# Gather of the expert rows with two float32r parts of x in place of three bf16 parts

## The chip, the core and the metric

The kernel runs on one core of one Trainium2 chip. The core has five engines that matter here: PE (TensorE, matrix products; PEld in the profile is its loading of the stationary operand), DVE (VectorE), ACT (ScalarE), POOL (GpSimd) and SP, whose queue issues the large loads. The metric is the device time of one execution in microseconds (us): 1502.05 us for the kernel before, the median of two runs (1501.78 and 1502.33 us).

## The reference

Two transformer layers are computed for two groups of 128 tokens each (g = 0 and g = 1), 1024 features wide. Each layer has an attention part and a mixture of experts. The change is in the second:

```python
s = jax.nn.sigmoid((t @ w_router).astype(jnp.float32))        # 256 tokens x 64 experts
...                                                           # top 4 groups of 8, then top 8 experts
hid = jax.nn.silu(jnp.einsum('td,edf->tef', t, w_gate)) * jnp.einsum('td,edf->tef', t, w_up)
routed = jnp.einsum('tef,efd->td', hid * gates[:, :, None].astype(hid.dtype), w_down)
shared = (jax.nn.silu(t @ ws_gate) * (t @ ws_up)) @ ws_down
```

There are 64 experts with a hidden width of 256. A token has a gate other than zero for 8 of them, so that the kernel needs to compute an expert for its own tokens only. All of it is float32.

## The kernel before

Each layer runs in stages: products for queries, keys and values; attention; the output product; the normalised row h of each token (`pre_norm`) and its transpose hT; the router; the shared expert; and the loop over the routed experts.

**Router.** PE multiplies hT by the router weights (L738), ACT takes the sigmoid (L998), and DVE chooses the experts in a chain of some 45 small instructions, each of which waits for the one before (L1246 to L1339). PE needs this chain twice: for the ranks (L744 to L748, which wait for the chosen mask, `mask_ready`), and for the list of visits (L753). Between them it works on the shared expert's first product (L758).

**The loop over visits.** Experts are handled in pairs. A visit takes one pair and up to 64 tokens for each expert (64 slots an expert, 128 in all). The profiled execution has 66 visits in the loops of the two layers. In one visit PE does, in this order (`visit`):

- `gate_up` (L814): the gathered rows of this visit by the gate and up weights;
- `gather` for the next visit (L789): the 128 chosen rows of x, transposed. The stationary operand is a 128x128 block of x (tokens by features), the moving one the choice of slots `pick` (tokens by 128 slots, ones and zeros). There are 8 blocks of features and 2 groups of tokens. x is float32, and stands as a sum of three bf16 parts in tile `x_parts` (name x3 in the code), so 8 x 2 x 3 = 48 products;
- two transposes of the hidden rows (L833), and `scatter` for the visit before (L806): 8 products of the float32r matrix `put` by the float32r parts y_hi and y_lo of the result;
- `scatter_prep` (L796, L798): transposes of pick for `put`, and the gates of the slots;
- the down product (L845).

DVE and ACT serve it: the gathered rows and the hidden rows are copied out of PSUM (L1380, L1021, L1377, L1023), `slots_of` makes `put` (L1352, L1355), `choose` builds `pick` for a later visit (L1345, L1347), and L1026 and L1387 split the result into y_hi and y_lo. SP loads 6 MB of weights for each visit, as three transfers of 2 MB, two visits ahead. The order of instructions on each engine is the order in which the code is written; semaphores tie the engines.

Two more gathers, one for each layer, stand ahead of the loops, so `gather` runs 68 times.

**The three parts of x** are made once a layer, between `pre_norm` and the loop: ACT rounds h to the first part (L990), POOL subtracts it from h in place (L483), ACT rounds the rest to the second part (`middle`, L995), POOL subtracts that and writes the third (L487). PE waits for all of it (`x3_ready`) ahead of the first gather.

Of the kernel before, what the change touches and what calls it, by code (L numbers as in the profile page):

```python
# [12 lines left out]
NG = 2  # L13
PAST = 128
P = 128
KT = D // P
# [17 lines left out]
SLOTS = 64  # L34
# [63 lines left out]
def program(nc, io):  # L98
# [6 lines left out]
    cursor = [base]  # L105
# [70 lines left out]
    x3 = sb("x_parts", [P, NG, 3, KT, P], bf16)  # L176
    xgT_at = cursor[0]
    xgT = sb("gathered", [P, 2, KT, P])
    pick = sb("pick", [P, 2, NG, 2 * SLOTS + 8], bf16)
    put = sb("put", [P, 2, NG * T], f32r)  # L180
# [21 lines left out]
    cursor[0] = max(experts_end, shared_region)  # L202
# [4 lines left out]
    cursor[0] = max(cursor[0], phase_end)  # L207
# [12 lines left out]
    cmp1 = sb("cmp1", [P, NG, 8, 8])  # L220

# [4 lines left out]
    with ctx:  # L226
        PS = ctx.enter_context(nc.psum_tensor("PS", [P, 8, HALF], f32))

        def sem(name):
            return ctx.enter_context(nc.semaphore(name))  # L230
# [26 lines left out]
        x_hi, x_rest, x_mid, x3_ready = sem("x_hi"), sem("x_rest"), sem("x_mid"), sem("x3_ready")  # L257
# [140 lines left out]
        def _(pool):  # L398
# [33 lines left out]
            for l in range(DEPTH):  # L432
# [46 lines left out]
                for g in range(NG):  # L479
                    blocks = h[:, g, :].rearrange("t (p j) -> t j p", j=KT)  # L480
                    pool.wait_ge(tr_mm, NG * (3 * l + 2) + g + 1)
                    pool.wait_ge(x_hi, NG * l + g + 1)
                    nc.gpsimd.tensor_tensor(blocks, blocks, x3[:, g, 0, :, :], ALU.subtract).then_inc(x_rest, 1)  # L483
                for g in range(NG):
                    blocks = h[:, g, :].rearrange("t (p j) -> t j p", j=KT)
                    pool.wait_ge(x_mid, NG * l + g + 1)
                    nc.gpsimd.tensor_tensor(x3[:, g, 2, :, :], blocks, x3[:, g, 1, :, :], ALU.subtract).then_inc(x3_ready, 1)  # L487
# [6 lines left out]
        def _(pe):  # L494
# [181 lines left out]
            for l in range(DEPTH):  # L676
# [106 lines left out]
                def gather(u, half):  # L783

                    for j in range(4):
                        jj = 4 * half + j
                        for g in range(NG):
                            for part in range(3):
                                last = mm(PS[:, 5 + half, j * P:(j + 1) * P], x3[:, g, part, jj, :], pick[:, u % 2, g, 0:P],  # L789
                                          start=(g, part) == (0, 0), stop=(g, part) == (1, 2), skip_group_check=True)  # L790
                    last.then_inc(S["ga_mm"], 1)
# [58 lines left out]
                pe.wait_ge(x3_ready, NG * (l + 1))  # L850
# [18 lines left out]
        def _(act):  # L869
# [81 lines left out]
            for l in range(DEPTH):  # L951
# [37 lines left out]
                for g in range(NG):  # L989
                    run(x3[:, g, 0, :, :], h[:, g, :].rearrange("t (p j) -> t j p", j=KT), ACT.Copy).then_inc(x_hi, 1)  # L990

                def middle(g):

                    act.wait_ge(x_rest, NG * l + g + 1)
                    run(x3[:, g, 1, :, :], h[:, g, :].rearrange("t (p j) -> t j p", j=KT), ACT.Copy).then_inc(x_mid, 1)  # L995
# [3 lines left out]
                for g in range(NG):  # L999
                    middle(g)  # L1000
# [31 lines left out]
        def _(dve):  # L1032
# [188 lines left out]
            for l in range(DEPTH):  # L1221
# [19 lines left out]
                rows_out(3 * l + 2)  # L1241

# [98 lines left out]
                def choose(u, visit):  # L1341

                    slots = RK[:, :, bass.ds(visit * 2, 2)].unsqueeze(3).to_broadcast([P, NG, 2, SLOTS])
                    iota = C["slot"].unsqueeze(1).unsqueeze(1).to_broadcast([P, NG, 2, SLOTS])
                    v.tensor_tensor(pick[:, u % 2, :, 0:P].rearrange("p g (e s) -> p g e s", e=2), iota, slots, ALU.is_equal)  # L1345
                    pair = visit & (PAIRS - 1)
                    v.tensor_copy(pick[:, u % 2, :, P:P + 6],  # L1347
                                  G3[:, :, :, :].rearrange("p g e k -> p g (e k)")[:, :, bass.ds(pair * 6, 6)]).then_inc(S["picked"], 1)
# [118 lines left out]
```

## Time and profile before

| | |
|---|---|
| median of two runs | 1502.05 us |
| profiled execution, device time | 1498.62 us |
| its span, first to last instruction | 1496.8 us |
| mean granted TensorE clock | 0.962 |
| loop of layer 0, about | 250 to 750 us of the span |
| loop of layer 1, about | 954 to 1486 us |
| PE busy, all lines | 1386.2 us |
| of it: gate and up (L814) | 464.5 us |
| of it: down (L845) | 241.1 us |
| of it: gather (L789), 3264 products | 194.0 us |

Times in the timeline count from the first instruction. The mean duration of a matmul is longer than the distance between two of them, because they are pipelined: the gather's products have a mean of 219 ns, but 48 of them take 2.85 us from the first start to the last end. Therefore the cost of a group is read from starts in the timeline, not from the mean. Full clock is 1.0 in the column PEclk (2.4 GHz), 0.5 is the lower level (1.2 GHz).

### The profile page before, as it was taken

What the parts mean: (1) busy time and instruction counts of PE and PEld (TensorE: products, weight loads), DVE (VectorE), ACT (ScalarE), POOL (GpSimd) and SP (SyncE); (2) the same over time, 40 slices, a digit from 0 to 9 for tenths busy, and PEclk for the clock granted to TensorE, in tenths of its full rate; (3) what the DMA queues carried; (4) which work ended last, traced back from release to release, by engine and by line L of the source; (5) the groups of instructions that cost most, each with busy time, mean ns of one, the idle gap of its engine ahead of it and who ended that gap; (6) DMA issues with size and microseconds to landing.
All of it is one profiled execution on the core that took longest, in us unless ns stands there. A gap on an engine that the chain in (4) does not pass through costs nothing.

```text
span 1496.8 us, 23839 instructions
## 1 busy us (share of the span) xinstructions
PE 1386.2 (93%) x9650; PEld 783.0 (52%) x9650; DVE 457.0 (31%) x982; ACT 339.5 (23%) x607; POOL 81.6 (5%) x97
## 2 busy tenths in 40 slices
PE   3797888999999999999979696999999999999996
PEld 1575654455454554545458574455454554545443
DVE  1534543222222222222263446322222222222223
ACT  1423451111111111111152354111111111111111
POOL 2011040000000000000020204000000000000000
PEclk7799979999999999999989897999999999999998
DMA  9589845999999999999657534799999999999991
GB/s 358 194 299 403 334 194 201 395 411 407 399 398 410 410 404 410 390 413 406 244 182 279 202 132 169 276 391 412 406 392 417 397 407 412 393 417 394 404 413 46
DMA packets 84831, 509.68 MB, mean 341 GB/s; under 512 B 4736, under 2 KB 4736, under 8 KB 33344
## 3 DMA queue, kind: packets, MB, share of 16 engines
q1 hardware_dynamic: 82960, 503.93, 84.1%
q0 software_dynamic: 1840, 5.31, 1.1%
q8 instruction: 22, 0.36, 0.1%
q14 instruction: 9, 0.07, 0.0%
HBM read 506.60 MB, written 2.62 MB: 340 GB/s over the span
## 4 chain that ended last, share of the span: by engine, by line
PE 86%; DVE 4%; DMA 4%; ACT 3%; issue 1%; POOL 1%; SPq 0%; POOLq 0%; ACTq 0%; DVEq 0%
PE PS L814 30%; PE PS L845 16%; PE PS L789 13%; PE PS L637 10%; PE PS L806 8%; DMA weights<-in_w_ada 2%; DMA weights<-in_w_out 2%; PE PS L833 1%; PE PS L758 1%; PE PS L659 1%; PE PS L778 1%; PE PS L738 1%; ACT weights_split L912 1%; DVE h L1121 1%; PE PS L796 1%
## 5 line engine op out<-in xcount | busy, mean ns | idle before, releaser
L814 PE MATMUL PS<-weights,gathered 128*64 128x512 f32 x2112 | 464.5, 592 | 0.0
L814 PEld LDWEIGHTS PS<-weights,gathered 128*64 128x64 f32 x2112 | 151.5, 137 | 301.9 <-issue 301.9
L845 PE MATMUL PS<-weights,hiddenT 128*64 128x512 f32 x1056 | 241.1, 598 | 0.0
L789 PEld LDWEIGHTS PS<-pick,x_parts 128*128 128x128 bf16 x3264 | 182.6, 98 | 54.7 <-issue 54.7
L789 PE MATMUL PS<-pick,x_parts 128*128 128x128 bf16 x3264 | 194.0, 219 | 0.0
L1377 DVE SCALAR_TENSOR_TENSOR hidden<-PS,slot_gate,silu 128x256 f32<-128x256 f32 x66 | 32.0, 485 | 410.5 <-ACT silu L1019 410.5
L1026 ACT ACTIVATE y_hi<-PS 128x512 fp32r<-128x512 f32 x132 | 78.9, 597 | 304.7 <-PE PS L845 304.7
L1387 DVE TENSOR_TENSOR y_lo<-PS,y_hi 128x512 fp32r<-128x512 f32 x132 | 91.3, 692 | 154.1 <-ACT y_hi L1026 154.1
L845 PEld LDWEIGHTS PS<-weights,hiddenT 128*64 128x64 f32 x1056 | 69.9, 136 | 114.5 <-issue 113.1
L637 PE MATMUL PS<-weights_split,hT_high 128*128 128x512 f32 x448 | 110.0, 401 | 14.7 <-ACT weights_split L912 8.9
L1019 ACT ACTIVATE silu<-PS 128x256 f32<-128x256 f32 x66 | 25.4, 384 | 429.7 <-PE PS L814 429.7
L637 PEld LDWEIGHTS PS<-weights_split,hT_high 128*128 128x128 f32 x448 | 85.7, 194 | 36.3 <-issue 9.3
L806 PE MATMUL PS<-y_hi,put 128*128 128x512 f32 x272 | 90.4, 413 | 2.8 <-DVE y_lo L1387 2.8
L806 PE MATMUL PS<-y_lo,put 128*128 128x512 f32 x272 | 84.8, 393 | 0.0
L1380 DVE COPY gathered<-PS 128x512 f32<-128x512 f32 x66 | 45.7, 692 | 123.7 <-PE PS L789 123.7
L415 POOL TENSOR_SCALAR rstd<-sum_squares 128x1 f32<-128x1 f32 x16 | 8.5, 529 | 1169.2 <-ACT h L919 1161.2
L659 PE MATMUL PS<-weights,c_columns 128*32 128x256 f32 x768 | 50.4, 418 | 16.1 <-DMA weights<-in_w_ada 16.1
L1062 DVE TENSOR_TENSOR weights_split<-weights,weights_split 128x4096 fp32r<-128x4096 f32 x14 | 61.6, 4420 | 12.1 <-ACT weights_split L912 12.1
L1352 DVE CAST put<-PS 128x256 fp32r<-128x256 bf16 x68 | 28.9, 425 | 107.1 <-PE PS L798 107.1
L806 PEld LDWEIGHTS PS<-y_lo,put 128*128 128x128 f32 x272 | 51.1, 188 | 11.5
L1021 ACT ACTIVATE gathered<-PS 128x512 f32<-128x512 f32 x66 | 39.4, 597 | 69.5 <-PE PS L789 69.5
L637 PE MATMUL PS<-weights_split,hT_low 128*128 128x512 f32 x224 | 53.1, 389 | 0.0
(227 smaller groups left out, 982.1 us busy)
## 6 DMA issues: line engine op xcount, KB each, us to landing
weights<-in_w_gate SPq DMA_DIRECT2D x66, 2048.0 KB, 9.8
weights<-in_w_up SPq DMA_DIRECT2D x66, 2048.0 KB, 14.2
weights<-in_w_down SPq DMA_DIRECT2D x66, 2048.0 KB, 11.1
weights<-in_w_ada SPq DMA_DIRECT2D x24, 2048.0 KB, 13.9
weights<-in_w_in SPq DMA_DIRECT2D x10, 2048.0 KB, 9.6
weights<-in_w_out SPq DMA_DIRECT2D x4, 2048.0 KB, 16.9
weights<-in_ws_gate SPq DMA_DIRECT2D x2, 1024.0 KB, 4.8
weights<-in_ws_up SPq DMA_DIRECT2D x2, 1024.0 KB, 6.9
```

Source lines behind the costliest of these rows:

```text
L637: last = mm(PS[:, banks[g], :], rows_[:, j, g, :], w[:, j * HALF:(j + 1) * HALF], start=start and j == 0, stop=w is lo and j == KT - 1, sk ...
L659: last = mm(PS[32 * q:32 * q + 32, bank, 0:QUARTER], cb[:, jj, :, :].rearrange("p g c -> p (g c)"), w[:, j, q * QUARTER:(q + 1) * QUARTER] ...
L789: last = mm(PS[:, 5 + half, j * P:(j + 1) * P], x3[:, g, part, jj, :], pick[:, u % 2, g, 0:P], start=(g, part) == (0, 0), stop=(g, part) = ...
L806: last = mm(PS[:, 2 * g + n, :], put[:, u % 2, g * T:(g + 1) * T], y[:, n * HALF:(n + 1) * HALF], start=False, stop=False, skip_group_chec ...
L814: last = mm(PS[64 * e:64 * e + 64, 4, :].rearrange("p (a n) -> p a n", a=2), xgT[:, b, j, 64 * e:64 * e + 64], w[:, e, :, j, :], start=j = ...
L845: last = mm(PS[64 * e:64 * e + 64, bank, :], hidT[:, j, 64 * e:64 * e + 64], w[:, e, j, n * HALF:(n + 1) * HALF], start=j == 0, stop=j == ...
L1021: run(*gathered(1 - b, 0), ACT.Copy).then_inc(S["xg_a"], 1)
L1026: run(yhi[:, n * HALF:(n + 1) * HALF], PS[:, bank, :], ACT.Copy).then_inc(S["yhi_done"], 1)
L1062: v.tensor_tensor(lo, w, hi.bitcast(f32), ALU.subtract).then_inc(w_low, 1)
L1377: v.scalar_tensor_tensor(hid[:, :], PS[:, 4, F:2 * F], slot_gate[:, b:b + 1], silu[:, :], ALU.mult, ALU.mult)\
L1380: v.tensor_copy(xgT[:, 1 - b, 4:8, :], PS[:, 6, :].rearrange("p (j s) -> p j s", j=4)).then_inc(S["xg_d"], 1)
L1387: v.tensor_tensor(ylo[:, cols], PS[:, bank, :], yhi[:, cols].bitcast(f32), ALU.subtract).then_inc(S["ylo_done"], 1)
```

## The change

x now stands as two float32r parts: ACT writes the first (the same place, L990 before), and DVE subtracts it from h and writes the second, right behind `rows_out` and ahead of the router's chain. POOL's four subtractions a layer and ACT's two `middle` roundings are gone. The gather takes both parts, so 8 x 2 x 2 = 32 products, and its moving operand is a new float32r tile `pick_rows`, built by DVE with one more instruction in `choose`. The bf16 `pick` stays for `scatter_prep`. A region of scratch for the router's tiles moves to an unused part of another tile; no wait goes with that.

```diff
--- before.py
+++ after.py
@@ -173,10 +173,11 @@
 
     phase_end = cursor[0]
     cursor[0] = shared_region
-    x3 = sb("x_parts", [P, NG, 3, KT, P], bf16)
+    x2 = sb("x_parts", [P, NG, 2, KT, P], f32r)
     xgT_at = cursor[0]
     xgT = sb("gathered", [P, 2, KT, P])
     pick = sb("pick", [P, 2, NG, 2 * SLOTS + 8], bf16)
+    pickr = sb("pick_rows", [P, 2, NG, 2 * SLOTS], f32r)
     put = sb("put", [P, 2, NG * T], f32r)
     y_at = cursor[0]
     yhi = sb("y_hi", [P, D], f32r)
@@ -199,12 +200,11 @@
     nmx = sb("pair_count", [P, PAIRS])
     act_ = sb("active", [P, VISITS])
     assert cursor[0] <= xgT_at + 8192
-    cursor[0] = max(experts_end, shared_region)
+    cursor[0] = mb_at + 4096
     incl = sb("active_sum", [P, VISITS])
     pos = sb("position", [P, VISITS])
     item = sb("item", [P, 4])
     wsum = sb("gate_sum", [P, 4])
-    cursor[0] = max(cursor[0], phase_end)
     s_ = sb("scores", [P, NG, N_EXP])
     sel = sb("sel", [P, NG, N_EXP])
     selm = sb("sel_masked", [P, NG, N_EXP])
@@ -218,6 +218,7 @@
     gm = sb("group_mask", [P, NG * N_EXP_GROUPS])
     top8 = sb("top8", [P, NG, 8])
     cmp1 = sb("cmp1", [P, NG, 8, 8])
+    assert cursor[0] <= mb_at + 16384
 
     C = {k: const[:, a:a + n] for k, (a, n) in where.items()}
     ident = C["ident"]
@@ -254,7 +255,7 @@
         nwt_mm, nwt_a, nwt_d, npv_mm, cat_done = sem("nwt_mm"), sem("nwt_a"), sem("nwt_d"), sem("npv_mm"), sem("cat_done")
         wo_mm, resid = sem("wo_mm"), sem("resid")
         w_high, w_low = sem("w_high"), sem("w_low")
-        x_hi, x_rest, x_mid, x3_ready = sem("x_hi"), sem("x_rest"), sem("x_mid"), sem("x3_ready")
+        x_hi, x_low = sem("x_hi"), sem("x_low")
         rlog_mm, s_ready, mask_ready, rank_mm = sem("rlog_mm"), sem("s_ready"), sem("mask_ready"), sem("rank_mm")
         item_ready, item_mm, table_ready = sem("item_ready"), sem("item_mm"), sem("table_ready")
         sh_mm, sh_silu, sh_hid, sht_mm, shT_ready = sem("sh_mm"), sem("sh_silu"), sem("sh_hid"), sem("sht_mm"), sem("shT_ready")
@@ -476,15 +477,6 @@
                 nc.gpsimd.memset(ylo[:, :].bitcast(f32), 0.0)
                 nc.gpsimd.memset(put[:, 1, :].bitcast(f32), 0.0)
                 nc.gpsimd.memset(slot_gate[:, :], 0.0).then_inc(cleared, 1)
-                for g in range(NG):
-                    blocks = h[:, g, :].rearrange("t (p j) -> t j p", j=KT)
-                    pool.wait_ge(tr_mm, NG * (3 * l + 2) + g + 1)
-                    pool.wait_ge(x_hi, NG * l + g + 1)
-                    nc.gpsimd.tensor_tensor(blocks, blocks, x3[:, g, 0, :, :], ALU.subtract).then_inc(x_rest, 1)
-                for g in range(NG):
-                    blocks = h[:, g, :].rearrange("t (p j) -> t j p", j=KT)
-                    pool.wait_ge(x_mid, NG * l + g + 1)
-                    nc.gpsimd.tensor_tensor(x3[:, g, 2, :, :], blocks, x3[:, g, 1, :, :], ALU.subtract).then_inc(x3_ready, 1)
                 root(4 * l + 3)
                 if l + 1 < DEPTH:
                     root(4 * l + 4)
@@ -785,9 +777,9 @@
                     for j in range(4):
                         jj = 4 * half + j
                         for g in range(NG):
-                            for part in range(3):
-                                last = mm(PS[:, 5 + half, j * P:(j + 1) * P], x3[:, g, part, jj, :], pick[:, u % 2, g, 0:P],
-                                          start=(g, part) == (0, 0), stop=(g, part) == (1, 2), skip_group_check=True)
+                            for part in range(2):
+                                last = mm(PS[:, 5 + half, j * P:(j + 1) * P], x2[:, g, part, jj, :], pickr[:, u % 2, g, :],
+                                          start=(g, part) == (0, 0), stop=(g, part) == (1, 1), skip_group_check=True)
                     last.then_inc(S["ga_mm"], 1)
 
                 def scatter_prep(u):
@@ -847,7 +839,7 @@
                                           skip_group_check=True)
                         last.then_inc(S["down_mm"], 1)
 
-                pe.wait_ge(x3_ready, NG * (l + 1))
+                pe.wait_ge(x_low, NG * (l + 1))
                 pe.wait_ge(S["picked"], 1)
                 for half in range(2):
                     gather(0, half)
@@ -987,17 +979,10 @@
                 rows_out(3 * l + 2)
                 act.wait_ge(kv_out, 64 * (l + 1))
                 for g in range(NG):
-                    run(x3[:, g, 0, :, :], h[:, g, :].rearrange("t (p j) -> t j p", j=KT), ACT.Copy).then_inc(x_hi, 1)
-
-                def middle(g):
-
-                    act.wait_ge(x_rest, NG * l + g + 1)
-                    run(x3[:, g, 1, :, :], h[:, g, :].rearrange("t (p j) -> t j p", j=KT), ACT.Copy).then_inc(x_mid, 1)
+                    run(x2[:, g, 0, :, :], h[:, g, :].rearrange("t (p j) -> t j p", j=KT), ACT.Copy).then_inc(x_hi, 1)
 
                 act.wait_ge(rlog_mm, l + 1)
                 run(s_[:, :, :], PS[:, 7, 0:NG * N_EXP].rearrange("p (g e) -> p g e", g=NG), ACT.Sigmoid).then_inc(s_ready, 1)
-                for g in range(NG):
-                    middle(g)
                 for g in range(NG):
                     act.wait_ge(sh_mm, NG * l + g + 1)
                     run(ssilu[:, g, :], PS[:, 2 + g, 0:F], ACT.Sigmoid).then_inc(sh_silu, 1)
@@ -1239,6 +1224,10 @@
                     finish_vector(7)
                 pre_norm(4 * l + 2, BCAST * (4 * l + 3))
                 rows_out(3 * l + 2)
+                for g in range(NG):
+                    blocks = h[:, g, :].rearrange("t (p j) -> t j p", j=KT)
+                    dve.wait_ge(x_hi, NG * l + g + 1)
+                    v.tensor_tensor(x2[:, g, 1, :, :], blocks, x2[:, g, 0, :, :].bitcast(f32), ALU.subtract).then_inc(x_low, 1)
 
                 dve.wait_ge(kv_out, 64 * (l + 1))
                 dve.wait_ge(router_in, 32 * (l + 1))
@@ -1342,6 +1331,7 @@
 
                     slots = RK[:, :, bass.ds(visit * 2, 2)].unsqueeze(3).to_broadcast([P, NG, 2, SLOTS])
                     iota = C["slot"].unsqueeze(1).unsqueeze(1).to_broadcast([P, NG, 2, SLOTS])
+                    v.tensor_tensor(pickr[:, u % 2, :, :].rearrange("p g (e s) -> p g e s", e=2), iota, slots, ALU.is_equal)
                     v.tensor_tensor(pick[:, u % 2, :, 0:P].rearrange("p g (e s) -> p g e s", e=2), iota, slots, ALU.is_equal)
                     pair = visit & (PAIRS - 1)
                     v.tensor_copy(pick[:, u % 2, :, P:P + 6],
```

**PE, one visit of the loop**, from `gate_up` to the down product (x_parts is x, pick or pick_rows the choice of slots, put the scatter matrix). Before:

```order
L814 MATMUL PS<-weights,gathered 64x512 x16
L826 REGISTER_ALU
L827 REGISTER_ALU
L789 MATMUL PS<-pick,x_parts 128x128 x48
L833 MATMUL PS<-const,hidden 128x128 x2
L806 MATMUL PS<-y_hi,put 128x512 x2
```

and with the change:

```order
L806 MATMUL PS<-weights,gathered 64x512 x16
L818 REGISTER_ALU
L819 REGISTER_ALU
L781 MATMUL PS<-pick_rows,x_parts 128x128 x32
L825 MATMUL PS<-const,hidden 128x128 x2
L798 MATMUL PS<-y_hi,put 128x512 x2
```

The gather stays in its place and has 32 products for 48; everything else on PE is as it was (line numbers are 8 to 10 lower).

**DVE, the last part of a visit.** Before:

```order
L1380 COPY gathered<-PS 128x512
L1352 CAST put<-PS 128x256
L1355 TENSOR_REDUCE slot_gate<-PS 64x1 x2
L1345 ISA
L1345 TENSOR_TENSOR pick<-const,slot_of 128x2x128
```

and with the change:

```order
L1370 COPY gathered<-PS 128x512
L1342 CAST put<-PS 128x256
L1345 TENSOR_REDUCE slot_gate<-PS 64x1 x2
L1334 ISA
L1334 TENSOR_TENSOR pick_rows<-const,slot_of 128x256
L1335 TENSOR_TENSOR pick<-const,slot_of 128x2x128
```

One instruction is added, ahead of `pick` and of the two y_lo subtractions that follow in both.

**POOL, behind the roots of the norm** (tiles cleared for the loop, then the parts of x, then the next root). Before:

```order
L477 MEMSET put 128x256
L478 MEMSET slot_gate 128x2
L483 TENSOR_TENSOR h<-h,x_parts 128x8x128 x2
L487 TENSOR_TENSOR x_parts<-h,x_parts 128x1024 x2
L415 TENSOR_SCALAR rstd<-sum_squares 128x1
```

and with the change:

```order
L478 MEMSET put 128x256
L479 MEMSET slot_gate 128x2
L416 TENSOR_SCALAR rstd<-sum_squares 128x1
```

POOL has no elementwise work left between the clearing and the next root.

## Rows read from the trace of the kernel before

**Rows 1.** The page: the chain that ended last, by engine and line.

```profile
PE 86%; DVE 4%; DMA 4%; ACT 3%; issue 1%; POOL 1%; SPq 0%; POOLq 0%; ACTq 0%; DVEq 0%
```

**Rows 2.** The timeline of PE, one visit (start us, us, what).

```profile
700.39 7.04 PE L814 MATMUL PS<-weights,gathered 128*64 128x512 f32 x32
707.36 2.85 PE L789 MATMUL PS<-pick,x_parts 128*128 128x128 bf16 x48
710.05 0.46 PE L833 MATMUL PS<-const,hidden 128*128 128x128 f32 x2
...
715.92 7.04 PE L814 MATMUL PS<-weights,gathered 128*64 128x512 f32 x32
```

**Rows 3.** Windows in the loop: PE, PEld, DVE, ACT, POOL busy us, PEclk, DMA share, GB/s.

```profile
490.00:505.50 15.50, 15.50 (x112) 7.86 (x111) 3.71 (x9) 2.56 (x5) 0.00 (x0) 1.00 1.00 415
...
567.50:583.00 15.50, 15.50 (x112) 7.89 (x110) 3.71 (x9) 2.56 (x5) 0.00 (x0) 1.00 0.98 397
```

**Rows 4.** Waits of SP's queue: total us, times, longest.

```profile
SPq L388 <- PE PS L845: 460.1, 62, 7.5
```

**Rows 5.** Groups by form on PEld: xcount | busy us, mean ns | idle.

```profile
L789 PEld LDWEIGHTS PS<-pick,x_parts 128*128 128x128 bf16 x3264 | 182.6, 98 | 54.7 <-issue 54.7
...
L806 PEld LDWEIGHTS PS<-y_lo,put 128*128 128x128 f32 x272 | 51.1, 188 | 11.5
```

**Rows 6.** Line L596, weight loads: duration ns min/median/max.

```profile
L596 PEld LDWEIGHTS PS<-U,probs x32: 186/192/333, 130.5 to 870.4; 128*128 128x128 f32 x32
```

**Rows 7.** The timeline of PE in attention.

```profile
161.97 0.39 PE L596 MATMUL PS<-cache_nv,probs 128*128 128x64 f32 x2
...
163.54 1.92 PE L501 MATMUL PS<-const,h 128*128 128x128 f32 x16
```

**Rows 8.** The timeline of PEld at the scatter.

```profile
710.22 0.32 PEld L806 LDWEIGHTS PS<-y_hi,put 128*128 128x128 f32 x2
```

**Rows 9.** The timeline at the router of layer 0.

```profile
209.89 4.07 ACT L990 ACTIVATE x_parts<-h 128x1024 bf16<-128x1024 f32 x2
...
217.96 0.29 DVE L1246 TENSOR_TENSOR sel<-scores,b_router 128x128 f32<-128x128 f32 x1 [7.87 <-ACT scores L998]
...
219.73 0.29 DVE L1259 TENSOR_TENSOR cmp<-group_score 128x128 f32<-128x128 f32 x1
219.86 5.30 POOL L487 TENSOR_TENSOR x_parts<-h,x_parts 128x1024 bf16<-128x1024 f32 x2 [2.38 <-ACT x_parts L995]
219.94 2.75 DVE L1260 TENSOR_TENSOR cmp<-group_score 128x128 f32<-128x128 f32 x1
222.72 2.59 DVE L1262 TENSOR_TENSOR cmp<-cmp,const 128x128 f32<-128x128 f32 x1
...
228.38 0.20 PE L744 MATMUL PS<-chosen,earlier 128*128 128x64 bf16 x1 [3.89 <-DVE chosen L1285]
...
228.54 7.95 PE L758 MATMUL PS<-weights,hT 128*128 128x512 f32 x14
```

**Rows 10.** Windows behind the chosen mask, layer 0 and layer 1; columns as above.

```profile
230.00:236.40 6.40, 6.40 (x12) 2.33 (x10) 5.07 (x25) 0.10 (x1) 0.00 (x0) 0.77 0.00 0
...
934.70:940.90 6.20, 6.20 (x19) 2.57 (x17) 5.70 (x31) 0.38 (x1) 0.00 (x0) 1.00 0.01 1
```

**Rows 11.** The timeline of layer 0, up to the first gather.

```profile
236.42 0.38 PE L753 MATMUL PS<-const,item 128*1 128x128 f32 x2
...
237.44 0.15 DVE L1347 COPY pick<-gate_parts 128x12 bf16<-128x12 bf16 x1
238.55 2.84 PE L789 MATMUL PS<-pick,x_parts 128*128 128x128 bf16 x48
```

**Rows 12.** The timeline at the router of layer 1.

```profile
934.56 0.20 PE L744 MATMUL PS<-chosen,earlier 128*128 128x64 bf16 x1 [3.70 <-DVE chosen L1285]
...
934.72 6.25 PE L758 MATMUL PS<-weights,hT 128*128 128x512 f32 x14
```

**Rows 13.** The timeline of DVE at the end of a visit.

```profile
713.24 0.42 DVE L1345 TENSOR_TENSOR pick<-const,slot_of 128x256 bf16<-128x256 f32 x1
...
715.05 0.69 DVE L1387 TENSOR_TENSOR y_lo<-PS,y_hi 128x512 fp32r<-128x512 f32 x1 [1.31 <-ACT y_hi L1026]
```

## Prediction

> **What bounds the kernel now.** I read the chain of waits first: 86% of the span ends on PE [rows 1]. The timeline of one visit shows the same: PE goes from `gate_up` to `gate_up` in 715.92 - 700.39 = 15.53 us without an idle time [rows 2], and in windows of the loop it is busy for 15.50 of 15.50 us at full clock [rows 3]. The same windows show a second resource that is almost full: the DMA engines are busy for 98 to 100% and move 397 to 415 GB/s. Which of the two is ahead is read from SP's queue: it waits for the down product 62 times, 460.1 us in all, up to 7.5 us at a time [rows 4], so transfers are asked for when PE lets go of a buffer, and PE does not wait for them. PE is the bound, with the transfers right behind it. A longer gather is therefore paid in full; a shorter one soon meets the transfers. Last I read the stretch around the router, where PE does wait: 3.89 us for the chosen mask in layer 0 [rows 9] and 3.70 us in layer 1 [rows 12].
>
> **The gather, 68 times.** Now it takes PE from 707.36 to 710.05, the start of the next product: 2.69 us for 48 products, 0.056 us each [rows 2]. At that pace 128 columns pass in 0.053 us at 2.4 GHz, so in bf16 the moving columns set the pace, and the weight loads are hidden: their mean is 98 ns, and they overlap [rows 5].
>
> The 32 new products have the same shape, but both operands are float32r, 4 bytes each. The trace has no float32r product with 128 moving columns; those of the scatter have 512. What it has is the weight load: in float32r with 128 columns one takes 188 ns against 98 for bf16 [rows 5]. With 512 moving columns there is room for that. The same load occurs with fewer columns in attention, on plain float32: 186 to 192 ns [rows 6], in front of 64 moving columns. There 14 products lie between 161.97 and 163.54 [rows 7]: 1.57 / 14 = 0.112 us each. In plain float32 a product is recorded as two instructions, and by the other rows such an instruction streams its columns twice (L814 below); 2 x 64 columns at 2.4 GHz are 0.053 us, half of what is seen. So there the pace is set by the loads, at 0.112 us. This is my price for a float32r product with 128 columns: its load is of the same size and length (188 and 192 ns), and its own stream of 0.053 us is hidden behind it.
>
> The bounds: from below 0.056 us, if the loads can be hidden as in bf16; from above 0.13 us, the distance of two float32r loads at the scatter (two of them in 0.32 us, the last 0.19 long [rows 8]), as far as the loads alone set it. A higher price needs another mechanism (rival C). I take 0.112, since the load's duration fits that row within 4 ns.
>
> So a gather takes 32 x 0.112 = 3.58 us, 0.89 more than 2.69. With 68 gathers (66 visits and one ahead of each loop) that is **+60.5 us**. At 0.13 it is 4.16, +100 us. Nothing hides it, since PE has no idle time in the visit [rows 2, 3]. The number of products in the other groups stays the same. L814 also gives the two-pass figure: 32 recorded instructions of 512 columns, two at a time on halves of the array, in 7.0 us, 0.44 us a pair [rows 2].
>
> The Trainium skill, TensorE: Matmul & The Clock Gate, section "Back-to-back issue gap", puts the distance of isolated matmuls at the moving columns over the clock plus some 2.5 ns, 56 ns for 128 columns, and names no type. The bf16 gather agrees with it (56 ns), the float32 rows do not (112 ns). By that rule 32 products would be 1.79 us and the change a gain; that is rival A. The same page, "Weight-path perf modes", says that the fast weight load is not used for FP32 inputs, and "LDWEIGHTS" gives columns / 1.2, 107 ns for 128 columns; by it the sum would be +50 us.
>
> **`choose` on DVE.** One more instruction with 256 elements, like `pick` at 0.42 us [rows 13]. In a visit it pushes the end of pick's group, and behind it the first y_lo subtraction, which today waits for 1.31 us on ACT's y_hi [rows 13]. 0.42 fits; 0. If ACT were earlier by an unexpected 0.9 us, DVE would be late by what is missing, under 0.4 us. The next `gate_up` and gather need `slot_gate` and the pick much later. Ahead of the loop, the first gather needs the pick: between 237.59 (end of the copy, 237.44 + 0.15) and 238.55 there is 0.96 us [rows 11]; 0.42 fits.
>
> **The parts of x, twice.** ACT's first rounding stays (209.89 to 213.96). DVE gets two subtractions of 1024 elements in the time when it waits for 7.87 us, until 217.96 [rows 9]. They have no row on DVE. Behind the rounding of the second group (213.96) there are 4.0 us for the last of them; POOL needs 5.30 / 2 = 2.65 us for such a one [rows 9], and DVE can be expected to need no more: 0. If it took twice that, 1.3 us a layer.
>
> POOL's subtractions go, and this is worth more than their own time. DVE's comparison L1259 takes 0.29 us, while the next two of the same shape take 2.75 and 2.59 us and end as POOL's two subtractions (219.86 to 225.16) end [rows 9]. Without POOL's work I price both at 0.29: the mask is 4.76 us earlier. PE waits for it for 3.89 and 3.70 us [rows 9, 12], so both waits go, and what is late next is PE's own work: **-7.6 us**. In layer 0 the 14 products behind the mask take 7.95 us, in layer 1 6.25 [rows 9, 12], at a granted clock of 0.77 and 1.00 [rows 10]. The drop came after the pause; with none I expect full clock: **-1.7 us**. The bounds are 0 and -9.5 us (twice 4.76). The list of visits (L753) comes after 14 products of PE in which DVE's chain has time.
>
> The Trainium skill, GPSIMD Engine Reference, section "Specifications", says that POOL shares its SBUF interfaces with VectorE and contends with DVE instructions that have two SBUF inputs. L1260 and L1262 agree; the tenfold price is only in the trace.
>
> ACT's two `middle` roundings lie behind the sigmoid, off PE's chain: 0.
>
> **The sum.** 1498.6 + 60.5 - 7.6 - 1.7 = 1549.8 us against the profiled execution. The median of the runs is 3.4 us above that execution (1502.05), so I expect **1553 us**, 3.4% more. A measurement here tells about 2% from no change, 30 us: the lines are 1472 and 1532.
>
> **Rivals.**
>
> A, faster than before: the float32r loads are hidden, a product costs its stream of 0.056 us, and a gather 1.79 us. PE's visit falls to 14.6 us. Then the transfers take over: at the best window's 415 GB/s the 6 MB (6.29 million bytes) need 15.2 us a visit, 0.37 less than now, 66 x 0.37 = 24 us. It gives 1502 - 9 - 24 = 1469 at best, 1484 if the present 15.4 (share 0.99) is the floor. For it: bf16 loads overlap. Against: float32 loads do not overlap so at 64 columns. The change is a gain below 2.69 / 32 = 0.084 us a product, before the router's gain. 0.10.
>
> B, in between: the load is partly hidden, 0.085 to 0.105 us, and the time is 1495 to 1538. No row is of that kind. 0.07.
>
> C, a short float32r stream is handled as plain float32, as two instructions' worth: L753 has 128 moving columns and a single weight column, two instructions in 0.38 us, of which the last is some 0.27 (0.108 a piece, 0.22 a product) [rows 11]. 32 x 0.22 = 7.0 us, +4.3 x 68 = +295, 1788 us. For it: nothing but the missing row at 128 columns. 0.07.
>
> D, the forecast, but POOL is not what held DVE (the two comparisons are slow in themselves): 9 us more, 1562; it is inside the forecast's range. That the change does not do what it says is excluded by the order: 32 products stand there, and the scatter's float32r products are recorded once each (8 a visit).
>
> **Chances and range.** The forecast (0.109 to 0.13 us, with or without the router's gain) has 0.74 and spans 1547 to 1602 us; something else that makes it slower has 0.02. To hold 8 in 10 I take 1512 to 1595: the forecast but its outer end, and the greater part of B. Faster by over 2%: 0.03 (A's best end). Within 2%: A's rest and most of B, 0.13. Slower: 0.84.
>
> **What the profile after should show.** The gather's 32 products in 3.5 to 4.2 us, and weight loads near 188 ns; a visit of 16.4 us with PE busy throughout; the DMA share in the loop near 0.94; L1260 and L1262 (ten lines earlier) at 0.29 us, and PE without a wait ahead of the ranks; y_lo still waiting for ACT, some 0.9 us. A gather near 1.8 us with PE waiting for weights would be A, one of 7 us C. If PE waits inside the visit for `picked` or for DVE, my zero for `choose` is wrong.

## The result

The changed kernel takes 1554.2 us (median of two runs, 1553.72 and 1554.67) against 1502.05 us: 3.5% slower, ratio 1.035 with a 95% interval from 1.032 to 1.038. The forecast was 1553 us. Measured again beside the experiments, the ratio was 1.039 (1.036 to 1.043).

The timeline of PE in the profile after shows one visit (start us, us, what); it answers to [rows 2]:

```profile
714.00 3.79 PE L781 MATMUL PS<-pick_rows,x_parts 128*128 128x128 f32 x32
717.62 0.47 PE L825 MATMUL PS<-const,hidden 128*128 128x128 f32 x2
...
730.48 3.79 PE L781 MATMUL PS<-pick_rows,x_parts 128*128 128x128 f32 x32
```

The gather takes 717.62 - 714.00 = 3.62 us for 32 products, 0.113 us each, where 48 products took 2.69. The visit is 730.48 - 714.00 = 16.48 us for 15.53, with no idle time between.

The group of the gather's loads on PEld (xcount | busy us, mean ns of one | idle), against [rows 5]:

```profile
L781 PEld LDWEIGHTS PS<-pick_rows,x_parts 128*128 128x128 f32 x2176 | 248.2, 192 | 54.5 <-issue 54.5
```

A load for the gather has gone from 98 to 192 ns, the length of the float32 loads of [rows 6].

The timeline at the router of layer 0, against [rows 9, 11] (L730 is the router's product, L750 the shared expert's, L736 the first of the ranks):

```profile
209.48 7.06 PE L730 MATMUL PS<-w_router,hT 128*128 128x64 f32 x32 [1.09 <-DVE hT L1032]
211.05 4.09 DVE L1230 TENSOR_TENSOR x_parts<-h,x_parts 128x1024 fp32r<-128x1024 f32 x2 [1.94 <-ACT x_parts L982]
...
216.33 8.55 PE L750 MATMUL PS<-weights,hT 128*128 128x512 f32 x14
...
216.99 0.29 DVE L1235 TENSOR_TENSOR sel<-scores,b_router 128x128 f32<-128x128 f32 x1 [1.84 <-ACT scores L985]
...
218.96 0.28 DVE L1249 TENSOR_TENSOR cmp<-group_score 128x128 f32<-128x128 f32 x1
219.28 0.29 DVE L1251 TENSOR_TENSOR cmp<-cmp,const 128x128 f32<-128x128 f32 x1
...
224.72 0.19 PE L736 MATMUL PS<-chosen,earlier 128*128 128x64 bf16 x1
...
224.87 6.25 PE L750 MATMUL PS<-weights,hT 128*128 128x512 f32 x14
...
232.78 4.08 PE L781 MATMUL PS<-pick_rows,x_parts 128*128 128x128 f32 x32
```

The two comparisons that took 2.75 and 2.59 us take 0.28 and 0.29. PE has no wait ahead of the ranks (L736), and the 14 products behind them take 6.25 us for 7.95. From the router's first product to the first gather PE now needs 232.78 - 209.48 = 23.30 us; before it was 238.55 - 210.45 = 28.10. In the kernel before, the router's first product in layer 0, and the same and the first gather in layer 1, are

```profile
210.45 7.06 PE L738 MATMUL PS<-w_router,hT 128*128 128x64 f32 x32 [1.09 <-DVE hT L1047]
...
916.63 7.06 PE L738 MATMUL PS<-w_router,hT 128*128 128x64 f32 x32 [1.09 <-DVE hT L1047]
...
943.03 2.84 PE L789 MATMUL PS<-pick,x_parts 128*128 128x128 bf16 x48
```

and in layer 1 after:

```profile
942.41 7.06 PE L730 MATMUL PS<-w_router,hT 128*128 128x64 f32 x32 [1.09 <-DVE hT L1032]
...
964.48 4.08 PE L781 MATMUL PS<-pick_rows,x_parts 128*128 128x128 f32 x32
```

So layer 1 needs 22.07 us for 26.40. Against that, in layer 0 the 14 products ahead of the ranks take 8.55 us for 7.18. Windows of the profile after (PE, PEld, DVE, ACT, POOL busy us, PEclk, DMA share, GB/s) show the clock there:

```profile
216.30:224.70 8.40, 8.40 (x16) 3.59 (x16) 6.23 (x40) 0.28 (x1) 0.00 (x0) 0.72 0.00 1
224.80:231.00 6.20, 6.20 (x20) 2.62 (x18) 5.47 (x28) 0.39 (x1) 0.00 (x0) 1.00 0.00 0
```

The granted clock in this stretch was 0.87 before and is 0.72 now. It is at its lower level through the whole of the router's products in both, and comes back between 219 and 220 us before, at 221 us after.

### The profile page after: what moved, and what is told of

Its sections match the earlier page's. It is cut to its first block, busy times and chain, and to the rows that moved or that the text cites. A ratio compares the mean times of both kernels' runs of the same rounds, so it can differ in the third digit from the quotient of the medians.

```text
span 1551.9 us, 21721 instructions
## 1 busy us (share of the span) xinstructions
PE 1450.3 (93%) x8562; PEld 847.3 (55%) x8562; DVE 479.3 (31%) x1056; ACT 331.8 (21%) x603; POOL 60.3 (4%) x89
## 4 chain that ended last, share of the span: by engine, by line
PE 88%; DMA 3%; ACT 3%; DVE 3%; issue 2%; POOL 1%; SPq 0%; POOLq 0%; ACTq 0%; DVEq 0%
PE PS L806 29%; PE PS L781 16%; PE PS L837 15%; PE PS L629 9%; PE PS L798 8%; PE PS L750 2%; DMA weights<-in_w_ada 2%; DMA weights<-in_w_out 1%; PE PS L825 1%; PE PS L651 1%; PE PS L770 1%; PE PS L730 1%; ACT weights_split L904 1%; DVE h L1106 1%; PE PS L788 1%
## 5 line engine op out<-in xcount | busy, mean ns | idle before, releaser
L781 PEld LDWEIGHTS PS<-pick_rows,x_parts 128*128 128x128 f32 x2176 | 248.2, 192 | 54.5 <-issue 54.5
L781 PE MATMUL PS<-pick_rows,x_parts 128*128 128x128 f32 x2176 | 258.3, 277 | 0.0
## 6 DMA issues: line engine op xcount, KB each, us to landing
weights<-in_w_up SPq DMA_DIRECT2D x66, 2048.0 KB, 14.1
weights<-in_w_ada SPq DMA_DIRECT2D x24, 2048.0 KB, 14.1
```

What stands on the lines that cost most here:

```text
L781: last = mm(PS[:, 5 + half, j * P:(j + 1) * P], x2[:, g, part, jj, :], pickr[:, u % 2, g, :], start=(g, part) == (0, 0), stop=(g, part) == ...
```

## The experiments

Twelve runs were made: ten further kernels, the kernel after once more (after_again) and one of the ten a second time. Several of them leave out a part of the gather, so that only their times are of use. "L" is the theory of the prediction: the load of the stationary operand sets the distance of the gather's products.

### What sets the price of a product

**Half of the moving columns** (moving_64), the kernel after with

```diff
-last = mm(PS[:, 5 + half, j * P:(j + 1) * P], x2[:, g, part, jj, :], pickr[:, u % 2, g, :],
+last = mm(PS[:, 5 + half, j * P:j * P + SLOTS], x2[:, g, part, jj, :], pickr[:, u % 2, g, 0:SLOTS],
```

> The kernel after, with only the first 64 of the 128 slot columns as moving operand of the gather (the other slots are not gathered, so half of the gathered rows are stale). Theory L, the load of 128 columns of 4-byte weights sets the distance: 32 products still take 3.6 us (0.113 each), the visit stays at 16.5 us and the time near 1554 us. Rival S, the float32r stream is slow by itself and costs in proportion to its columns: 0.056 us each, 1.8 us for 32, the visit falls to 14.7 us or to what the transfers allow (15.2 to 15.4), about 1475 to 1485 us.

It took 1687.85 us (one run). The timeline of PE:

```profile
694.43 3.76 PE L781 MATMUL PS<-pick_rows,x_parts 128*128 128x64 f32 x32
698.03 0.60 PE L825 MATMUL PS<-const,hidden 128*128 128x128 f32 x2
698.28 1.20 PE L798 MATMUL PS<-y_hi,put 128*128 128x512 f32 x2
...
712.48 4.46 PE L781 MATMUL PS<-pick_rows,x_parts 128*128 128x64 f32 x32
716.75 0.70 PE L825 MATMUL PS<-const,hidden 128*128 128x128 f32 x2
```

At full clock 32 products lie between 694.43 and 698.03, 0.1125 us each, though each streams half of what it did. This is what L says; the rival S, in which the price goes with the columns, has 1.8 us for the 32. But the total agrees with neither: the gather at 712.48 needs 4.27 us, and the scatter behind the first one has its first two products in 1.20 us for 0.70. Windows of the same run (columns as above) show the clock:

```profile
710.00:715.00 5.00, 5.00 (x35) 3.10 (x31) 0.48 (x1) 0.90 (x2) 0.00 (x0) 1.00 0.81 269
715.00:720.00 5.00, 5.00 (x21) 4.41 (x21) 0.69 (x1) 0.47 (x2) 0.00 (x0) 0.53 0.96 397
720.00:725.00 5.00, 5.00 (x23) 1.90 (x23) 2.18 (x7) 0.60 (x1) 0.00 (x0) 0.78 0.95 401
```

PE is never idle, and yet the granted clock falls from 1.00 to its lower level toward the end of the gather, and comes back in the down product.

The same kernel **once more** (moving_64_again) and one with 96 columns (**moving_96**, `pickr[:, u % 2, g, 0:96]` and 96 output columns) asked whether that was a disturbance:

> The kernel of moving_64 once more (the first 64 of the 128 slot columns alone, half of the gathered rows stale). There the distance of the products at full clock was 0.112 us as in the kernel after, but the granted clock fell in the gather and the time was 1688 us. Theory H, the clock answers to how little the array streams while it waits for loads: again a mean clock near 0.88 and 1650 to 1700 us. Rival N, it was a disturbed run: mean clock 0.966 and 1554 us.

> The kernel after with the first 96 of the 128 slot columns as moving operand of the gather (a quarter of the gathered rows stale). Theory L (loads set the distance): 0.112 us and 3.6 us for 32 where the clock is full. Theory H (the clock falls with little streaming): if it goes with the streamed share, 96 columns lie between 128 (mean clock 0.966, 1554 us) and 64 (0.876, 1688 us), 1554 to 1640 us. Rival N: 0.966 and 1554 us.

The first gave 1684.58 us, ratio 1.122 (1.117 to 1.128), mean clock 0.880. The second gave 1598.9 us (one run), mean clock 0.930 over the run, and 0.113 us a product where the clock is full:

```profile
661.74 3.78 PE L781 MATMUL PS<-pick_rows,x_parts 128*128 128x96 f32 x32
665.35 0.49 PE L825 MATMUL PS<-const,hidden 128*128 128x128 f32 x2
```

So it was no disturbance (N falls), and H, the theory that the clock answers to the products, has its forecasts met: with 128, 96 and 64 columns at the same distance of products, the mean clock is 0.966, 0.930 and 0.88, and the time 1554, 1599 and 1685 to 1688 us. A smaller product made the kernel slower by 130 us. The number of visits is 66 in all of them (2112 records of the gate and up products); what changes is their length. From start to start of `gate_up` a visit takes 16.48 or 18.0 us with 96 columns, and 16.49, 18.0 or 19.57 us with 64, where it is 16.48 or 16.49 us with 128. Stale or wrong values among the gathered rows do not by themselves lower the clock: moving_256 and weights_64 below have them as well, and the mean clock there is 0.970 and 0.963.

**Twice the moving columns** (moving_256), both token groups' slots side by side, into 256 output columns:

```diff
+last = mm(PS[:, 5 + half, (j % 2) * 2 * P:(j % 2 + 1) * 2 * P], x2[:, g, part, jj, :], pickr[:, u % 2, :, :].rearrange("p g s -> p (g s)"),
```

> The kernel after, with 256 moving columns in each product of the gather (the slot columns of both token groups side by side), the same number of products and the same weights; what is gathered is then wrong. Theory L: a stream of 256 columns is 0.107 us at full clock, still just under the load, so the distance rises only a little, to 0.113 to 0.122 us (float32r with 512 columns shows 13 ns above its stream): 3.6 to 3.9 us for 32, time 1554 to 1573 us. Rival S: twice the columns, 0.226 us, 7.2 us for 32, the visit 20.1 us, about 1798 us.

```profile
708.66 7.04 PE L806 MATMUL PS<-weights,gathered 128*64 128x512 f32 x32
715.63 4.04 PE L781 MATMUL PS<-pick_rows,x_parts 128*128 128x256 f32 x32
719.50 0.41 PE L825 MATMUL PS<-const,hidden 128*128 128x128 f32 x2
725.33 7.04 PE L806 MATMUL PS<-weights,gathered 128*64 128x512 f32 x32
```

Twice the work in 3.87 us for 3.62: 0.121 us a product (0.117 to 0.118 between two starts). L holds. The visit grew by 0.19 us to 16.67. The total, 1597.24 us, is above what was expected for another reason: the gather's records number 2240 for 2176, which is two visits more, 33 us. Both are in layer 1 (36 visits for 34; layer 0 has 32 in both), where the router works on the wrong results of layer 0.

**Half of the stationary columns** (weights_64):

```diff
-last = mm(PS[:, 5 + half, j * P:(j + 1) * P], x2[:, g, part, jj, :], pickr[:, u % 2, g, :],
+last = mm(PS[0:64, 5 + half, j * P:(j + 1) * P], x2[:, g, part, jj, 0:64], pickr[:, u % 2, g, :],
```

> The kernel after, with only 64 of the 128 columns of each stationary block of x in the gather (the other 64 rows of each block stay stale). Theory L: the load halves, to about 137 ns in its record as in the expert products with 64 columns, and the distance falls to 0.056 to 0.07 us, 1.8 to 2.2 us for 32. PE's visit would be 14.7 to 15.0 us, and then the transfers set it: 15.2 to 15.4 us a visit, about 1470 to 1485 us. Rival S and any fixed price of a float32r product: the distance stays 0.113 us and the time 1554 us.

```profile
652.07 2.14 PE L781 MATMUL PS<-pick_rows,x_parts 128*64 128x128 f32 x32
...
666.89 2.14 PE L781 MATMUL PS<-pick_rows,x_parts 128*64 128x128 f32 x32
```

With the same 128 moving columns and half of the load, 32 products need (2.14 - 0.22) / 31 = 0.062 us each, about half of 0.113; the 0.22 us is the mean of one product. Together with the runs before, this shows L: with 128 stationary columns the price follows the load and not the stream. The time was 1442.24 us, less than the 1470 expected at the lowest: the floor that I had put on the transfers is not there. The visit is 666.89 - 652.07 = 14.82 us.

**Fewer columns in bf16** (bf16_96): the kernel before with `x3[:, g, part, jj, 0:96]` and 96 output partitions.

> The kernel before, with only 96 of the 128 columns of each stationary bf16 block of x in the gather (the other 32 rows of each block stay stale). Theory F, a bf16 load is short only in a fast form that needs all 128 columns (the Trainium skill, TensorE: Matmul & The Clock Gate, section Weight-path perf modes; no row shown so far bears on it): the load takes 160 to 170 ns in its record and the distance rises to about 0.083 us, 4.0 us for 48 and 1.3 us more a visit, about 1585 us. Rival B2, the load simply costs by bytes, 2 for 4: 96 columns are shorter or equal, the distance stays at 0.056 us, 2.69 us for 48, time 1499 to 1502 us.

```profile
707.34 2.88 PE L789 MATMUL PS<-pick,x_parts 128*96 128x128 bf16 x48
710.06 0.45 PE L833 MATMUL PS<-const,hidden 128*128 128x128 f32 x2
```

2.72 us for 48 products, 1500.93 us beside 1499.52 (one run each): no change, so F's price is wrong and B2's is right. B2's reason, a cost by bytes, is not: one load has a record of 123 ns, longer than the 98 ns of a load with 128 columns, as F had it, though not by as much. The fast form that the Trainium skill describes (TensorE: Matmul & The Clock Gate, section "Weight-path perf modes") fits these two records, but a bf16 load without it is hidden here as well.

### What fewer products bring, and where the transfers bind

**Two bf16 parts** (two_bf16), the kernel before with x rounded to two parts, 16 bits for 24:

```diff
-for part in range(3):
+for part in range(2):
```

> The kernel before, with the third bf16 part left out of the gather's products (it is still made), so x is rounded to two parts: 32 products as in the kernel after, but in bf16. It asks what the number of products alone brings, and where the transfers take over (rival A of the prediction). Theory: 32 x 0.056 = 1.79 us for 2.69, PE's part of a visit 14.6 us, but the 6 MB of weights need 15.2 us at 415 GB/s, so PE waits for weights 0.5 to 0.8 us a visit and the time is 1478 to 1495 us, 0.5 to 1.6% under the kernel before. Rival: the transfers have room that the windows do not show, the visit is 14.6 us, and the time 1442 us.

1444.15 us, ratio 0.963 (0.960 to 0.965): below the whole range of the theory (1478 to 1495), and within 2 us of the rival's 1442. The theory of a floor at 15.2 us falls.

```profile
644.78 7.04 PE L814 MATMUL PS<-weights,gathered 128*64 128x512 f32 x32
...
659.42 7.04 PE L814 MATMUL PS<-weights,gathered 128*64 128x512 f32 x32
```

The visit is 659.42 - 644.78 = 14.64 us. PE does not wait here, and the windows show more than the 415 GB/s that I had taken as the most:

```profile
490.00:505.00 15.00, 15.00 (x98) 6.99 (x94) 3.72 (x9) 2.56 (x5) 0.00 (x0) 1.00 1.01 422
505.00:520.00 15.00, 15.00 (x97) 7.01 (x95) 3.71 (x9) 2.56 (x5) 0.00 (x0) 1.00 1.02 424
```

**One bf16 part** (one_bf16), `range(1)`, x rounded to 8 bits:

> The kernel before with only the first bf16 part of x in the gather's products (x is rounded to 8 bits): 16 products, 0.9 us. It looks for the floor of the transfers that rival A of the prediction put at 15.2 us a visit and that two_bf16 passed at 14.64 us with PE never waiting. PE's part of a visit would be 13.75 us, which asks for 6.29 million bytes / 13.75 us = 458 GB/s. Theory: the transfers cannot do that; the windows of two_bf16 show 421 to 424 GB/s at a share of 1.01, so the visit ends at 14.4 to 14.9 us, PE waits for weights ahead of the gate and up products, and the time is 1430 to 1450 us. Rival: they can, the visit is 13.75 us and the time about 1383 us.

1445.93 us, and here PE waits:

```profile
643.62 7.09 PE L814 MATMUL PS<-weights,gathered 128*64 128x512 f32 x32 [0.54 <-DMA weights<-in_w_up]
...
658.73 7.09 PE L814 MATMUL PS<-weights,gathered 128*64 128x512 f32 x32 [0.92 <-DMA weights<-in_w_up]
...
673.45 7.09 PE L814 MATMUL PS<-weights,gathered 128*64 128x512 f32 x32 [0.56 <-DMA weights<-in_w_up]
```

From 643.62 to 673.45 two visits take 14.92 us each, 422 GB/s. That is the floor of the transfers: from 300 to 680 us of its span the windows show 421 to 422 GB/s throughout. Two_bf16 runs 0.3 us a visit below it because the weights are asked for two visits ahead. The rows of its w_up transfers (KB each, median us from issue to landing), between 250 and 450 us of the span and between 550 and 750 us, are

```profile
weights<-in_w_up SPq DMA_DIRECT2D x14, 2048.0 KB, 15.3
...
weights<-in_w_up SPq DMA_DIRECT2D x10, 2048.0 KB, 20.3
```

The queue grows through the loop, and the lead lasts almost as long as the loop with its 32 or 34 visits: over both loops the weight loads of `gate_up` wait for w_up for 2.7 us in all, PE for 0.2 us, and each of these waits is near a loop's end (the first at 673 us). In the kernel before the same median is 14.3 and 14.1 us.

### The router's part

**The parts on DVE** (dve_parts): the kernel before with its gather and its three parts, but

```diff
-                    nc.gpsimd.tensor_tensor(blocks, blocks, x3[:, g, 0, :, :], ALU.subtract).then_inc(x_rest, 1)
...
+                    v.tensor_tensor(blocks, blocks, x3[:, g, 0, :, :], ALU.subtract).then_inc(x_rest, 1)
...
+                    v.tensor_tensor(x3[:, g, 2, :, :], blocks, x3[:, g, 1, :, :], ALU.subtract).then_inc(x3_ready, 1)
```

with the third part's subtraction gone from POOL too, and `middle` ahead of the sigmoid.

> The kernel before with its three bf16 parts and its gather, but the four subtractions that make the parts moved from POOL to DVE ahead of the router's chain, and ACT's two middle roundings moved ahead of the sigmoid. It is the router's part of the change without the gather's. Theory P, POOL's subtractions held DVE's two comparisons: both take 0.29 us and PE's wait ahead of the ranks goes, but the chain starts some 2 us later than in the kernel after, which is about its slack. Router to gather 28.1 and 26.4 us before become 23 to 24 and 21 to 23 us, in all 6 to 9 us less: 1493 to 1496 us against 1502, ratio 0.994 to 0.996. Rival Q, the comparisons are slow in themselves: they stay at 2.6 to 2.8 us, and the later start makes it 2 to 8 us slower than before.

1494.67 us, ratio 0.997 (0.995 to 0.998). In its profile both comparisons take 0.28 to 0.29 us, and PE waits 1.18 us for the mask, since the chain starts later. Router to gather takes 23.85 us in layer 0 and 23.84 in layer 1, for 28.10 and 26.40: 6.8 us less, at the low end of the 6 to 9 expected. Layer 1 is above its 21 to 23, and the ratio a little above its 0.994 to 0.996: of the 6.8 us of the profile the medians show 4.6. Q falls.

**POOL's work given back** (pool_back), the kernel after with

```diff
+pool.wait_ge(s_ready, l + 1)
+for g in range(NG):
+    step(nc.gpsimd.tensor_tensor(yhi..., blocks, x2[:, g, 0, :, :].bitcast(f32), ALU.subtract))
```

> The kernel after, with two subtractions of 1024 elements (h minus the first part, into a tile that is cleared afterwards) given back to POOL right behind the sigmoid, where the kernel before had them; nobody needs their result, and they feed no wait of the chain. Theory P: DVE's comparisons are held again to 2 to 3 us each while POOL works, the mask is 4 to 5 us later, PE waits 2 to 4 us ahead of the ranks in each layer, and the time is 4 to 9 us above the kernel after: 1558 to 1563 us. Rival Q: the comparisons stay at 0.29 us and the time at 1554 us.

1561.24 us beside 1556.61 for the kernel after (**after_again**, the same batch):

> The kernel after, unchanged, on the same chip as the three beside it. All theories: ratio to the kernel before 1.035, about 1554 us, a visit of 16.49 us.

```profile
218.44 6.06 POOL L483 TENSOR_TENSOR y_hi<-h,x_parts 128x1024 fp32r<-128x1024 f32 x2 [11.92 <-ACT scores L991]
218.75 1.19 DVE L1245 MAX8 top_of_group<-sel 128x8 f32<-128x8 f32 x16
219.97 1.49 DVE L1247 TENSOR_TENSOR group_score<-top_of_group 128x16 f32<-128x16 f32 x1
221.50 0.29 DVE L1254 TENSOR_TENSOR cmp<-group_score 128x128 f32<-128x128 f32 x1
221.71 2.94 DVE L1255 TENSOR_TENSOR cmp<-group_score 128x128 f32<-128x128 f32 x1
224.56 0.95 POOL L485 MEMSET y_hi<- 128x1024 f32 x1
224.68 0.29 DVE L1257 TENSOR_TENSOR cmp<-cmp,const 128x128 f32<-128x128 f32 x1
...
228.05 0.20 PE L742 MATMUL PS<-chosen,earlier 128*128 128x64 bf16 x1 [2.12 <-DVE chosen L1280]
```

Each of POOL's two subtractions holds one DVE instruction with two inputs until it ends: first group_score, 1.49 us for 0.19, then a comparison, 2.94 us for 0.28. The comparison at 221.50 us, which starts together with the second subtraction, and the one beside POOL's clearing, which reads nothing, take 0.29; MAX8, with one input, takes 1.19 beside the subtraction and 1.18 without. PE waits again, 2.12 us here and 2.60 in layer 1. The intervals of the ratios, 1.038 to 1.043 and 1.036 to 1.043, overlap, so that the 4.6 us between the medians are not shown by the times alone; the traces show 26.89 and 26.60 us from the router to the gather, for 23.30 and 22.07.

**Both findings together** (two_bf16_dve), two bf16 parts, the second from one subtraction on DVE, and no `middle`:

```diff
+v.tensor_tensor(x3[:, g, 1, :, :], blocks, x3[:, g, 0, :, :], ALU.subtract).then_inc(x3_ready, 1)
```

> x as two bf16 parts (16 bits of it in place of 24), multiplied as in two_bf16, and the second part made by DVE in one subtraction ahead of the router's chain, so that POOL's subtractions and ACT's middle roundings go as in the kernel after. If the two findings add, the gather's share is that of two_bf16 (ratio 0.963 to the kernel before) and the router's share that of the kernel after (8 to 9 us less, with the smaller gather ahead of the loops): 1434 to 1440 us, ratio 0.957 to 0.960, the comparisons at 0.29 us and a visit of 14.64 us. Rival: with POOL's work gone the expert weights are asked for earlier and something else binds, then 1440 to 1445 us.

1432.96 us, ratio 0.954 (0.950 to 0.957), a little under the forecast, and the fastest of all. Its x has 16 bits, where the kernel before has 24; with 24 bits, dve_parts is the fastest.

## Why the prediction was right

**The gather.** Forecast 0.112 us a product and +60.5 us; measured 0.113 us, 0.93 us more a gather, 68 x 0.93 = +63 us. The row that I chose (64 moving columns of plain float32 in attention) gave the price to 1%, because it has the same load and a stream that cannot hide it. Its "14 products" are 14 recorded instructions, two to a product; the instruction, with one load each, is what compares with a float32r product, and so the price is right. The three experiments with fewer and more columns show that this is the cause and not only a number that fits: 64, 96, 128 and 256 moving columns cost 0.112, 0.113, 0.113 and 0.121 us, and half a load costs 0.062.

**The router.** Forecast -7.6 and -1.7, together -9.3 us. Measured from the router's first product to the gather: -4.80 us in layer 0 and -4.33 in layer 1, together -9.1. The sum is right, and layer 0 in it is not: the 3.89 us of waiting and the 1.7 us behind it came, but 1.4 us went back, since the products ahead of the ranks ran at a lower mean clock (0.72 for 0.87). In layer 1 the wait (3.70) went and some 0.6 us more.

So layer 0 came out 0.8 us short of its part of the forecast and layer 1 0.6 us over; that the two nearly cancel is luck. The clock ahead of the ranks differs from execution to execution also where the router is as before: these 14 products take 7.18 us in the profile before, 7.31 in two_bf16, 8.42 in bf16_96 and 8.72 in one_bf16, and PE's wait for the mask is 3.89, 3.76, 2.65 and 2.37 us, so that the ranks start 17.9 us behind the router's first product each time. The wait took up what the clock cost; without the wait PE pays for it. So 3.89 us was the wait of one execution and no fixed price. Why the clock comes back later in some executions is open. The 1.7 us behind the mask has better support: the products there take 6.25 us in layer 0 of after and after_again, without a wait, and 7.95 and 7.55 us in the two layers of pool_back, behind its waits of 2.12 and 2.60 us; but behind the 3.70 us of layer 1 before they took 6.25 as well, so not every wait is followed by the drop.

That POOL held DVE was read from two rows; pool_back and dve_parts show it from both sides, so rival D is out.

**`choose` and the parts on DVE**, both forecast at 0. The timeline of DVE in the profile after:

```profile
720.83 0.43 DVE L1334 TENSOR_TENSOR pick_rows<-const,slot_of 128x256 fp32r<-128x256 f32 x1
...
722.64 0.69 DVE L1377 TENSOR_TENSOR y_lo<-PS,y_hi 128x512 fp32r<-128x512 f32 x1 [0.97 <-ACT y_hi L1011]
```

The new instruction takes 0.43 us and y_lo still waits for ACT for 0.97 us, where it was 1.31. The two subtractions take 4.09 us (POOL needed 5.3) and end 1.84 us before the chain begins.

**The ledger of the two spans**: +63 for the gathers, -9 for the router, and about +1 for the rest (0.02 to 0.03 us a visit, less a router that starts 1 us earlier in layer 0) make 1551.9 - 1496.8 = 55.1 us.

The sum stood for the profiled execution first, 1549.8 us; that one took 1553.72, 3.9 us more: 2.7 from the gathers, 0.2 from the router and 1 from the rest. The 1553 us for the median came out 1.2 us under the measured 1554.2 only because 3.4 us were added for the distance of the median from the profiled execution, and that distance was 0.5 us this time. So close a median is luck too; the gather's price is not.

**What was wrong** did not enter the forecast. Rival A's floor of 15.2 us a visit, from the best window's 415 GB/s, is refuted: the transfers can do 422 to 424, a lead of two visits carries the kernel below even that, and fewer products in bf16 brought 3.7% and not at most 2%. I also expected the DMA share to fall to 0.94 with the longer visit. It is at 0.97 with 380 GB/s, between 500 and 700 us: the share hardly falls with the load, so it could not tell how much room there was. Nor does SP's wait [rows 4] tell it: 460.1 us before, and still 362.9 us in one_bf16, at the floor. The landing times do: they stay at 14 us through the loop of the kernel before, and grow in two_bf16. Rival C is excluded by 0.113 us, and B by the same.

## What to carry to other kernels

Price a short product by the longer of its stream and its weight load. Take the load from a row of the same type in which nothing hides it, and there from the distance of two starts, not from the length of the record (192 ns for a distance of 0.112 us; in bf16 the records are 98 and 123 ns, and the distance is 0.056 us with both). Here 128 columns of 4-byte weights cost 0.112 us, twice a bf16 product, so that 32 such products cost more than 48 in bf16. Before POOL is given elementwise work, look at what DVE does at that time, since a two-input instruction there can take ten times as long. A wait in one profile may hide a cost that differs from run to run, so its removal need not give back its whole length. And a DMA share near 1.0 does not show a floor by itself; landing times that grow through a loop, or a wait of the consumer, do.

## What the runs showed of the hardware

- With 4-byte stationary operands, a product with 128 stationary columns starts 0.112 to 0.113 us after the one before, whether 64, 96 or 128 columns are streamed, and 0.117 to 0.118 us after it with 256 (at full clock). With 64 stationary and 128 moving columns it is about 0.06 us. The records of the loads are 192 and 135 ns (with 128 and 64 columns); in bf16 they are 98 ns with 128 columns and 123 ns with 96.
- TensorE's granted clock fell from its level of 2.4 GHz to that of 1.2 GHz while the engine had no idle time. In kernels that differ in the moving columns of the gather alone, the mean clock was 0.966 with 128, 0.930 with 96 and 0.88 with 64, and the time 45 and 130 us more.
- DVE instructions with two inputs in SBUF were held by POOL's two-input subtraction until that one ended, comparisons of 0.29 us for 2.6 to 2.9 us, and not at all by POOL's clearing (0.29 us). MAX8, with one input, was not held (1.19 us).
- A backlog of transfers of 0.3 us a visit stayed hidden through nearly the whole of a loop of 32 to 34 visits (0.2 us of waiting on PE), with median landing times that grew from 15.3 to 20.3 us.
